# A two-layer hybrid transformer block: squares summed while the residual is updated, and the scan's first tile, masks and weights prepared one stage earlier

## The reference, cut to what matters

```python
def reference(...):
    ...
        mod = (c_s @ ada_w[layer] + ada_b[layer])[:, None, :]
        sh1, sc1, g1, sh2, sc2, g2 = jnp.split(mod, N_MOD, axis=-1)
    ...
        hl = rmsnorm(x, norm_mix_w[layer]) * (1.0 + sc1) + sh1
        hc = rmsnorm(xc, norm_mix_w[layer]) * (1.0 + scc1) + shc1
        y_l, y_c = mixer(hc, hl, cos, sin, w_in[layer], ret_rate[layer], ret_norm_w[layer],
    ...
        x = x + g1 * y_l
        x = x + g2 * swiglu(rmsnorm(x, norm_ffn_w[layer]) * (1.0 + sc2) + sh2,
                            w_ffn_in[layer], w_ffn_out[layer])
    ...
    return rmsnorm(x, final_norm_w)
```

## Time and profile before

| what | us |
|---|---|
| time, median of 3 runs (lowest to highest) | 3844.21 (3841.21 to 3849.33) |
| the profiled execution: its own time | 3844.28 |
| the profiled execution: its span | 3842.4 |
| stage `frt` of layer 0 | 40.7 to 464.3 |
| `met`, `win`, `scn` of layer 0 | 472.7 to 584.4, 592.7 to 763.4, 764.3 to 913.0 |
| `mix`, `ffn` of layer 0 | 983.6 to 1103.6, 1104.8 to 2063.2 |
| `frt` of layer 1 | 2064.1 to 2479.9 |
| `met`, `win`, `scn` of layer 1 | 2488.0 to 2603.7, 2610.0 to 2759.3, 2760.2 to 2894.6 |
| `mix`, `ffn` of layer 1 | 2952.9 to 3048.3, 3049.5 to 3810.2 |
| `fin` | 3811.0 to 3842.4 |
| busy: PE, DVE, ACT, POOL | 3414.2, 1618.0, 1056.1, 660.3 |

### The profile page before, as it was taken

How to read it: one execution, slowest core, us unless ns; L and a number is a source line. 1 busy time by engine, 2 the same in 40 slices (tenths; PEclk the granted TensorE clock), 3 DMA queues, 4 the chain that set the end, 5 groups by cost and what they waited for, 6 DMA issues and landing times. The chain is left out here.

```text
span 3842.4 us, 56889 instructions
## 1 busy us (share of the span) xinstructions
PE 3414.2 (89%) x21948; PEld 2828.8 (74%) x21948; DVE 1618.0 (42%) x2653; ACT 1056.1 (27%) x1931; POOL 660.3 (17%) x764
## 2 busy tenths in 40 slices
PE   6989857878889999999998989757887889999998
PEld 3878646766758888888886878646775678888885
DVE  4465676632242322223236465675533233322234
ACT  3343135512132121121213243135512231122112
POOL 1133753222000000000001142753221000000000
PEclk8989868988899999999999999968997999999999
DMA  4456283096301111111111456283295011111111
GB/s 170 143 187 201 71 274 103 15 282 204 136 17 38 38 38 38 38 38 38 38 39 76 143 187 201 79 274 89 70 259 181 33 38 49 49 49 49 46 47 61
DMA packets 245757, 396.43 MB, mean 103 GB/s; under 512 B 76099, under 2 KB 148035, under 8 KB 245190
## 3 DMA queue, kind: packets, MB, share of 16 engines
q1 hardware_dynamic: 239750, 374.05, 30.9%
q0 software_dynamic: 5824, 19.93, 1.4%
HBM read 280.30 MB, written 101.52 MB: 99 GB/s over the span
## 5 line engine op out<-in xcount | busy, mean ns | idle before, releaser
L905 PE MATMUL ffn_bank<-ffn_h_hi,ffn_w_hi 128*128 128x512 f32 (+1 forms) x1760 | 650.6, 370 | 18.1 <-DVE ffn_h_lo L323 18.1
L908 PE MATMUL ffn_bank<-ffn_h_lo,ffn_w_hi 128*128 128x512 f32 (+1 forms) x1760 | 650.0, 369 | 0.0
L909 PE MATMUL ffn_bank<-ffn_h_hi,ffn_w_lo 128*128 128x512 f32 (+1 forms) x1760 | 649.5, 369 | 0.0
L815 PE MATMUL frt_acc<-frt_w_hi,frt_h_hi 128*128 128x472 f32 x960 | 375.5, 391 | 47.7 <-DVE frt_w_lo L695 26.0
L905 PEld LDWEIGHTS ffn_bank<-ffn_h_hi,ffn_w_hi 128*128 128x128 f32 x1760 | 333.3, 189 | 75.8 <-DVE ffn_h_lo L323 18.1
L909 PEld LDWEIGHTS ffn_bank<-ffn_h_hi,ffn_w_lo 128*128 128x128 f32 x1760 | 333.0, 189 | 55.6
L908 PEld LDWEIGHTS ffn_bank<-ffn_h_lo,ffn_w_hi 128*128 128x128 f32 x1760 | 333.2, 189 | 55.2
L899 DVE TENSOR_TENSOR ffn_w_lo<-ffn_raw,ffn_w_hi 128x1024 fp32r<-128x1024 f32 x132 | 161.7, 1225 | 503.1 <-ACT ffn_w_hi L895 497.9
L815 PE MATMUL frt_acc<-frt_w_hi,frt_h_lo 128*128 128x472 f32 x960 | 368.6, 384 | 0.0
L815 PE MATMUL frt_acc<-frt_w_lo,frt_h_hi 128*128 128x472 f32 x960 | 366.0, 381 | 0.0
L905 PE MATMUL ffn_bank<-ffn_a_hi,ffn_w_hi 128*128 128x512 f32 (+1 forms) x880 | 324.4, 369 | 0.8 <-DVE ffn_a_lo L973 0.8
(11 more groups left out here) (332 smaller groups left out, 5492.5 us busy)
## 6 DMA issues: line engine op xcount, KB each, us to landing
ffn_raw<-w_ffn SPq DMA_DIRECT2D x132, 512.0 KB, 3.5
x<-ada_w SPq DMA_DIRECT2D x15, 2048.0 KB, 9.3
proj<-frt_out SPq DMA_DIRECT2D x120, 236.0 KB, 2.0
x<-proj SPq DMA_DIRECT2D x60, 384.0 KB, 4.5
frt_raw<-w_in SPq DMA_DIRECT2D x96, 236.0 KB, 4.4
pack<-frt_side SPq DMA_DIRECT2D x80, 256.0 KB, 2.5
met_pr<-proj SPq DMA_DIRECT2D x20, 704.0 KB, 6.3
met_vn<-pack SPq DMA_DIRECT2D x20, 640.0 KB, 6.4
```

What stands on the lines that cost most here:

```text
L815: mm = pe.matmul(acc[q % NA][:, 0:GW], a[:, k, tok], b[:, k, :], start=(k == 0 and i == 0), stop=(k == KC - 1 and i == 2))
L905: mm = pe.matmul(out, w_hi, b_hi, start=first, stop=False)
L908: pe.matmul(out, w_hi, b_lo, start=False, stop=False)
L909: return pe.matmul(out, w_lo, b_hi, start=False, stop=last)
```

## The change

It has five parts. (1) A class `Squares`: in `mixed` and in the last phase of `ffn`, ACT squares each piece of `x` behind DVE's addition, and DVE adds it up over the 8 chunks in a new tensor `total` (128 x 1280), which lives until the next norm has read it. (2) `normed_from` takes the place of `normed` in both feed-forward stages and in the second layer's front, and the final stage is made likewise: PE turns `total` into sums with tokens on partitions (`sums`, two columns per tile), ACT takes one root and DVE one reciprocal of 20 or 16 columns, DVE lays them on diagonals into `total`, and PE spreads each slice over the partitions into PSUM (`spread`), from which the scale reads. The first layer's front keeps the old norm. (3) In the feed-forward stage the first turn goes slice by slice (`pe_first`) and follows chunk by chunk; the front's `project` does too. The weights' first remainders move behind the diagonals and behind the first slice. (4) The masks, the decay of a tile and the group totals are made in `meet`. (5) `EarlyTile.load` in the window stage brings 16 transfers instead of 6, the scan's whole tile 0 and its first half matrix of `ada_w`, and the scan no longer loads these; its loads start with tile 1.

```diff
+def normed_from(nc, st, x, total, scale, mod, shift0, lo, hi_t, lo_t, ones, eps, ident, scaled, spread, sums):
...
+    def pe_norm(pe):
+        for g in range(lo // P, TILES):
+            mm = pe.matmul(sums[:, 2 * g:2 * g + 2], total[:, g * P:(g + 1) * P], ones[:, 0:2], start=True, stop=True)
+        mm.then_inc(summed, 1)
+        for s, (t0, n) in enumerate(slices):
+            pe.wait_ge(laid, s + 1)
+            pe.matmul(spread[s][:, 0:n], ones[:], total[:, t0:t0 + n], start=True, stop=True).then_inc(spread_s, 1)
+
+    def act_norm(act, first=None, second=None):
+        act.activation(warm[:], eps[:], ACT.Sqrt)
+        act.wait_ge(summed, 1)
+        act.activation(root[:, whole, :], sums[:, 2 * whole.start:2 * TILES].rearrange("p (g a) -> p g a", a=2), ACT.Sqrt, bias=eps[:]).then_inc(rooted, 1)
...
+    def dve_norm(dve, first=None, second=None):
+        dve.wait_ge(rooted, 1)
+        dve.reciprocal(root[:, whole, :], root[:, whole, :]).then_inc(inverted, 1)
+        dve.wait_ge(inverted, 1)
+        for s, (t0, n) in enumerate(slices):
+            g, each = tiles(s), [P, n // P, P]
+            dve.scalar_tensor_tensor(total[:, t0:t0 + n].rearrange("p (g n) -> p g n", n=P), ident.unsqueeze(1).broadcast_to(each), float(DM),
+                                     root[:, g, 0:1].broadcast_to(each), ALU.mult, ALU.mult).then_inc(laid, 1)
...
+            first(dve)
+
...
+        def scale_one(i):
+            s, k = i // KC, i % KC
+            t0, n = slices[s]
+                dve.wait_ge(spread_s, s + 1)
+            if i >= 2:
+                dve.wait_ge(h_ready, i - 1)
+            dve.scalar_tensor_tensor(scaled[i % 2][:, 0:n], x[:, k, t0:t0 + n], scale[:, k, v:v + 1], spread[s][:, 0:n],
+                                     ALU.mult, ALU.mult).then_inc(scaled_s, 1)
+
...
+            if i == KC - 1 and second:
+                second(dve)
...
+    def square(self, act, m, s):
...
+        j = i - len(self.slices)
+        if j >= 2:
+            act.wait_ge(self.gathered, j - 1)
+        to = self.total[:, t0:t0 + n] if m == 0 else self.scratch[j % 2][:, 0:n]
+        act.activation(to, self.x[:, m, t0:t0 + n], ACT.Square).then_inc(self.squared, 1)
+
+    def gather(self, dve, m, s):
+        t0, n = self.slices[s]
+        i = m * len(self.slices) + s
+        j = i - len(self.slices)
+        if m:
+            dve.wait_ge(self.squared, i + 1)
+            dve.tensor_tensor(self.total[:, t0:t0 + n], self.total[:, t0:t0 + n], self.scratch[j % 2][:, 0:n], ALU.add).then_inc(self.gathered, 1)
...
-                    if g == 0:
-                        pe.wait_ge(h_ready, (1 + sum(t * P >= t0 + n for t0, n in slices)) * KC)
+                    at = sum(t * P >= t0 + n for t0, n in slices)
                     if q >= NA:
                         wait_copied(pe, q - NA)
                     for k in range(KC):
                         if t == 0:
                             pe.wait_ge(w_split, g * KC + k + 1)
+                        if g == 0:
+                            pe.wait_ge(h_ready, at * KC + k + 1)
                         for a, b, i in ((h_hi, w_hi, 0), (h_lo, w_hi, 1), (h_hi, w_lo, 2)):
                             mm = pe.matmul(acc[q % NA][:, 0:GW], a[:, k, tok], b[:, k, :], start=(k == 0 and i == 0), stop=(k == KC - 1 and i == 2))
...
+        def pe_first(pe):
+            for s, (t0, ln) in enumerate(slices):
+                for u in range(2):
+                    if s == 0:
+                        pe.wait_ge(w.ready[u], 1)
+                    for k in range(KC):
+                        if u == 0:
+                            pe.wait_ge(h_ready, s * KC + k + 1)
+                        f = slice(k * P, (k + 1) * P)
+                        begun = w.used[1] if u == 0 and s == 0 and k == 0 else w.used[0] if u == 1 and s == NS - 1 and k == 0 else None
+                        mm = three_passes(pe, bank[u][s][:, 0:ln], w.hi[u][:, f], w.lo[u][:, f],
+                                          h_hi[:, k, t0:t0 + ln], h_lo[:, k, t0:t0 + ln], k == 0, k == KC - 1, begun)
+                    mm.then_inc(full[u][s], 1)
+
...
-                if more:
+                        if last:
+                            if behind:
+                                squares.gather(dve, *behind)
+                            behind = (m, s)
+                if not last:
                     w.rest(dve, u, n + 1)
...
-                act_norm(act, between=lambda act: w.round(act, 0, 0))
-                w.round(act, 1, 0)
+                act_norm(act, first=lambda act: w.round_first(act, 0), second=lambda act: w.round_first(act, 1))
...
-                w.rest(dve, 0, 0)
-                dve_norm(dve)
-                w.rest(dve, 1, 0)
+                dve_norm(dve, first=lambda dve: w.rest(dve, 0, 0), second=lambda dve: w.rest(dve, 1, 0))
...
+                pe_norm(pe)
+                pe_first(pe)
...
                 plain(0)
+                act.wait_ge(s["fars"], 4)
+                for d in range(2):
+                    for h in range(4):
+                        act.activation(eg[:, d, h, :], far[:, d, :], ACT.Exp, scale=lg[:, 4 * d + h:4 * d + h + 1]).then_inc(s["egs"], 1)
+                act.activation(cd[:].rearrange("p d a q -> p (d a q)"), lg[:], ACT.Exp, scale=float(P)).then_inc(s["cds"], 1)
                 first(0)
                 second(0)
...
+                    if t == 0:
+                        dve.wait_ge(s["egs"], 8)
+                        dve.wait_ge(s["fars"], 4)
+                        dve.tensor_tensor(eg[:], eg[:], keep[:].unsqueeze(2).broadcast_to([P, 2, 4, P]), ALU.mult).then_inc(s["kept"], 1)
+                        dve.wait_ge(s["kept"], 1)
+                        dve.tensor_tensor(early.mask, eg[:, 0], eg[:, 1], ALU.add).then_inc(s["masked"], 1)
+                        dve.wait_ge(s["cds"], 1)
+                        for p in range(2):
+                            dve.tensor_copy(early.cdh[side_of(p)], cd[side_of(p), :, :, p]).then_inc(s["cdhs"], 1)
...
+                sp.dma_start(self.u_i[c][r, :], self.us[tt][r, 256 * d:256 * d + 256]).then_inc(landed, 16)
                 sp.dma_start(self.kaz[c][r, d, :], self.pack[tt][r, T_D + 512 * d:T_D + 512 * d + 512]).then_inc(landed, 16)
+            sp.dma_start(self.rkv[:, d, :], self.pack[tt][:, T_RK + 256 * d:T_RK + 256 * d + 512]).then_inc(landed, 16)
+        for p in range(2):
+            r = slice(64 * p, 64 * p + 64)
+            sp.dma_start(self.rqz[r, :, p, :], self.feat[0][r, F_RQ:F_RQ + 2, :]).then_inc(landed, 16)
+        sp.dma_start(self.rk, self.feat[0][:, F_RK:F_RK + 2, :]).then_inc(landed, 16)
+        sp.dma_start(self.w, self.ada).then_inc(landed, 16)
+
...
-                features(0)
-                sp.wait_ge(s["zeroed"], ZEROED)
-                retention(0)
                 m.sync_small(sp)
                 features(1)
+                sp.wait_ge(s["zeroed"], ZEROED)
                 keys(1)
                 retention(1)
-                m.sync_load(sp, 0)
                 features(2)
                 keys(2)
                 m.sync_load(sp, 1)
...
+                pool.memset(R[:], 0.0).then_inc(s["zeroed"], 1)
-                pool.memset(R[:], 0.0).then_inc(s["zeroed"], 1)
-                pool.memset(one[:], 1.0).then_inc(s["const"], 1)
-                pool.wait_ge(s["gths"], 2); pool.wait_ge(s["cdhs"], 2); pool.wait_ge(s["zeroed"], ZEROED)
+                pool.wait_ge(s["zeroed"], ZEROED)
...
+                for u in range(2):
+                    w.round(act, u, 0)
+                for m in range(KC):
+                    for s in range(NS):
+                        act.wait_ge(free[m % 2][s], m // 2 + 1)
+                        squares.square(act, m, s)
+                    if m + 2 < KC:
+                        w.round(act, m % 2, m // 2 + 1)
 
...
```

326 lines of the change are left out of this document (190 added, 136 removed).

## The result

The changed kernel takes 3792.9 us (median of 4 runs, 3788.9 to 3797.8) against 3842.7 for the kernel before (4 runs); the ratio is 0.9877, 95% interval 0.9861 to 0.9892. That is some 50 us faster (47 by the ratio), 1.2% where 2.6% was forecast. The forecast was 99 us and a range of 3722 to 3776 us: the direction held, the size did not, and the time lies outside the range.

A forecast was written before the change was run, and what follows sets the result against it. TensorE, 89% busy, was taken to bound the kernel, with gains only where it stands still. Terms 26.5 + 22.5 + 13.5 + 11 + 19 + 17 - 6.5 - 0.3 - 4.4 + 0.7 = 99; 3844.2 - 99 = 3745 us, range 3722 to 3776.

The forecast's parts named there:

- The three kinds of hole: TensorE stands still in the norms, in the scans waiting for `scn_rkv` (23.4 and 15.5 us), and in the 31.4 us last stage.
- The first turns: Feed-forward stages: first turn falls from 75.0 to 48.5 us in layer 0, 62.65 to 39.9 in layer 1; saves 26.5 and 22.5.
- The fourth tile of the second front: Layer 1's front: fourth tile starts 43 us after the stage's start, before 56.7; saves 13.5 us (9.5 to 19).
- A settled turn takes 1207.32 - 1179.76 = 27.56 us: Feed-forward, layer 0: length of a later turn, measured before the change; gave 5.5 us for half of the last 512-token slice.
- The window's term: First window stage: 16 transfers instead of 6 make POOL 6 us late for `q_first`; costs 6.5 us (4 to 10).
- The scans' terms: Scans: loads come 18.2 us earlier and cover waits; saves 19 us in layer 0 (11 to 26), 17 in layer 1 (11 to 18).
- The sign that I had named for this: Scans, new profile: TensorE's waits for `scn_rkv` are at most 5 us.
- Rival B: Scans stay DMA-bound, only bytes count: 6 to 11 us per scan, 3764 us; chance 0.13 shared with another rival.
- Meet: Meet stage: Exp and mask work ahead of the swap's addition delays VectorE; costs 2.2 us per layer (1 to 3).
- Rival A: VectorE against POOL: a scale reading PSUM escapes contention, front wins 3 us more, 3741 us; chance 0.09.
- Rival C: Norms: TensorE stays at 1.2 GHz, losing 3 to 5 us in each of four places, 3760 us; chance 0.07.
- Rival D: Mixing stage: squares queued on ACT delay rounding, TensorE runs dry at 16 units; slower, 3858 us at 7 us each; chance 0.03.

The follow-up runs named there:

- e1: Changed kernel with an unused tensor of 896 bytes per partition ahead of the feed-forward weight buffers, restoring their address modulo 2048: 3755.9 us, one run.
- e4: Kernel before the change with an unused tensor of 1152 bytes per partition ahead of the feed-forward weight buffers, placing them as in the changed kernel: 3865.7 us.
- e11: Changed kernel with weights re-placed, window's 2 MB behind the fourth block's queries, and scan 2 MB loads behind the next tile's retention loads: 3744.7 us, ratio 0.9741.

## Why the prediction was wrong, step by step

**Right.** The three kinds of hole were the right ones. The first turns: forecast 48.5 us after the start, measured 46.3; layer 1, 39.9 and 38.3. The fourth tile of the second front: forecast 43 us after the start, measured 2097.68 - 2056.4 = 41.3. The last stage: 19.0 and 19.5. The delay in the meet stage: 2.2 and 2.3. No wait for `mix_w_lo` came up in the middle of the mixing stages; the one at their start is 8.8 and 8.7 us, and was 8.8 before. That a price would be paid in the first window was right too.

**The step that failed.** "A settled turn takes 1207.32 - 1179.76 = 27.56 us" was measured before and used for after, and the section on what bounds the kernel said that a change which touches no matmul in the large phases can only win where TensorE stands still. It can also lose where TensorE runs. The change altered the sizes of what is allocated ahead of the weight buffers, that altered the distance between weights and activations, and all 66 weight units of each layer's feed-forward stage became slower, 1.7% by the turn in layer 0 (28.04 us instead of the 27.56 used) and 2.9% by the matmul in layer 1: 15 and 20 us (the stages of the changed kernel less those of e1) of the some 50 that are missing. No term stood for it, no rival named it and nothing in the range allowed for it; the covered cases were all about waits. e1 and e4 show it from both sides. With that repaired, the same change measured 3755.9 us in one run, inside the range.

**Mis-sized.** The window's term was -6.5 and measured -12.1: the wait was 9.6 us where I had 6, since the queries were there 634.35 - 598.6 = 35.7 us after the stage's start, where I had 624 - 592.7 = 31.3. Of the other 2.5 us the half-clock stretch behind the wait explains the most: the matmuls were busy for 5.6 us from 636.3 to 642.0 at a granted clock of 0.52, about 2.7 us more than at full clock (an estimate from these numbers; over the whole stage the same 1520 matmuls were busy 155.8 us instead of 153.0). The range had allowed for such a stretch, the term had not. The scans' terms were 19 and 17 and measured 14 each: I let 18 us of earlier loads cancel the waits one for one, while the 2 MB loads issued ahead of each tile's retention data kept making new ones (e11, in the first scan). The sign that I had named for this failed: the waits for `rkv` are 13.5 and 10.5 us in all, the longest 6.2, where they were to be at most 5. Rival B, the scan that stays bound by DMA, had 6 to 11 us for each scan: the measured 14 lie between it and me, and 7 of them in layer 1 are no waits at all. Meet was -2.2 twice; in layer 0 the stage shows -6.8, of which the runs settle only the 2.3 at its start. Adding up the low ends of the terms gives 66.7, so 3777.5 and not 3776 for the top of the range; nothing hangs on it.

**The weighed rule.** Rival A asked whether a scale that reads PSUM escapes POOL. Before, scale and remainder took 1.29 and 0.79 us beside POOL. After (timeline of the second front, VectorE and POOL):

```profile
2066.76 0.48 DVE L397 SCALAR_TENSOR_TENSOR frt_side<-x,amix,frt_b_s 128x256 f32<-128x256 f32 x1
2067.16 0.90 DVE L409 SCALAR_TENSOR_TENSOR frt_h_lo<-frt_side,mod,frt_h_hi 128x256 fp32r<-128x256 f32 x1
...
2066.33 1.44 POOL L754 TENSOR_TENSOR frt_w_lo<-frt_raw,frt_w_hi 128x472 fp32r<-128x472 f32 x1
```

The scale takes its uncontended 0.48 us while POOL works, the remainder, with two inputs in SBUF and begun within POOL's operation, 0.90. (A remainder that begins just ahead of POOL's takes 0.48 too, as at 2068.49, with POOL's at 2068.57.) This is what the Trainium skill's page "SBUF — State Buffer", section "Who interferes with whom", says of instructions with at most one and with two SBUF inputs. The fourth tile came 15.4 us earlier instead of the 13.5 I took from the middle. The stage as a whole won only 11.9: behind the fourth tile it took 3.5 us longer than before, 2.5 of them in the busy time of the same 1928 matmuls (346.1 instead of 343.6 us, granted clock 0.96 instead of 0.97); why is open.

**Rival C** (a colder clock in the norm) did not show as a loss at the four starts: the first 46 us of the first feed-forward stage had a granted clock of 0.85, where it was 0.82. It was 0.82 in the second feed-forward stage's norm, 0.77 in the second front's (0.92 before) and 0.55 in the last stage (0.78), but the first turns and the fourth tile came earlier than forecast (the tile after a wait of 7.55 us for ACT's copy), and the last stage ended 0.5 us later than forecast. **Rival D** did not occur.

## What to carry to other kernels

When a change alters what is allocated, compare the start addresses of the matmuls' operands before and after, and keep a pad at hand: here the same matmuls started 226.7 or 233.3 ns apart. If a saving at the start of a stage is seen and is gone at its end, count instructions per stretch of time before looking for waits. And a big load that leaves a crowded stage should be queued behind whatever its new neighbours need next, which was worth 8 us in the first window and 9 in the first scan, by one profile each.

## What was unexpected of the hardware

- The interval between 512-wide fp32r matmuls of the feed-forward stages, each with its weight load, depends on the distance modulo 256 bytes between the start addresses of stationary and moving data: 226.7 ns at 0, 233.3 at 32, 233.2 at 64, 233.3 at 128, 228.8 at 192 (up to 0.9 ns comes from something else). The intervals of 256-wide ones go otherwise: 119.6 at 0, 117.8 at 64, 118.4 at 128, and at 192 once 113.3 and twice 117.8. In the front, with 472 columns, distance 0 gave 211.1 ns in one layout and 213.3 in another.
- Less waiting went with a higher granted clock at the start of the scans: 0.77 instead of 0.52 in layer 0, 0.84 instead of 0.59 in layer 1. And a wait of 9.6 us in the window stage had a stretch of 13.7 us at the half level around it.
- Single profiles of the meet stage differ by up to 6.6 us between kernels that have the same code in it.
